# Gate and up projections as seven half products for eight, tokens in two groups, on one core

## The reference, cut to what matters

```python
def rmsnorm(x, g):
    r = lax.rsqrt(jnp.mean(xf * xf, axis=-1, keepdims=True) + EPS)
    return xf * r * g

def swiglu(hn, w_gate_up, w_down):
    gate, up = jnp.split(hn @ w_gate_up, 2, axis=-1)
    return (jax.nn.silu(gate) * up) @ w_down

h = h + swiglu(rmsnorm(h, norm_ffn_g), w_gate_up, w_down)
return rmsnorm(h, norm_final_g)
```

## Time and profile before

| | us |
|---|---|
| median of 3 runs | 2632.27 |
| lowest and highest | 2631.83, 2634.83 |
| the profiled execution: time | 2631.12 |
| the profiled execution: span from its first to its last instruction | 2629.4 |
| PE busy | 2526.4 |
| DVE busy | 1284.7 |
| ACT busy | 546.5 |
| POOL busy | 283.7 |

### The profile page before, as it was taken

The page is one execution under the profiler, slowest core; times in us unless marked ns, Lnnn a source line. Parts: engine busy times, 40 slices in busy tenths (PEclk is TensorE's granted clock), DMA queues, the critical chain, the costliest instruction groups (busy, mean ns, idle before and its releaser), DMA issues.

```text
span 2629.4 us, 31047 instructions
## 1 busy us (share of the span) xinstructions
PE 2526.4 (96%) x11282; PEld 2056.1 (78%) x11282; DVE 1284.7 (49%) x2113; ACT 546.5 (21%) x733; POOL 283.7 (11%) x238
## 2 busy tenths in 40 slices
PE   6899999799999999999999999999999999999994
PEld 4688887688888788888768888888888888888883
DVE  6634553368880784352442554434434434433437
ACT  5301110322221432130331321111111111111122
POOL 3278870000000220000000000000000000000001
PEclk9999999999999999999999999999999999999997
DMA  5432227532226642222310000000000000000002
GB/s 191 133 117 99 86 74 156 146 122 80 80 80 168 200 175 76 84 96 80 104 57 32 32 33 32 33 32 32 32 32 32 32 32 32 32 32 32 32 16 96
DMA packets 87288, 201.27 MB, mean 77 GB/s; under 512 B 12608, under 2 KB 41792, under 8 KB 87232
## 3 DMA queue, kind: packets, MB, share of 16 engines
q1 hardware_dynamic: 83872, 189.01, 22.2%
q0 software_dynamic: 3360, 11.54, 1.4%
HBM read 148.64 MB, written 53.97 MB: 77 GB/s over the span
## 4 chain that ended last, share of the span: by engine, by line
PE 90%; DVE 3%; DMA 2%; issue 2%; POOL 1%; ACT 1%; SPq 0%; DVEq 0%; POOLq 0%; ACTq 0%
PE bank L616 28%; PE bank L617 28%; PE bank L618 28%; PE bank L893 2%; PE bank L839 1%; PE bank L870 1%; DMA BBL<-scratch_BB 1%; POOL ACC L515 1%; DMA scratch_CO<-COS 1%; DVE HR L1774 1%; PE bank L836 0%; DVE ACC L1613 0%; PE bank L713 0%; PE bank L882 0%; PE bank L781 0%
## 5 line engine op out<-in xcount | busy, mean ns | idle before, releaser
L616 PE MATMUL bank<-XN,WLO 128*128 128x512 f32 x2400 | 935.5, 390 | 3.1 <-DVE XN L1711 1.7
L617 PE MATMUL bank<-XN,WHI 128*128 128x512 f32 x2400 | 933.8, 389 | 0.0
L618 PE MATMUL bank<-XN,WHI 128*128 128x512 f32 x2400 | 933.7, 389 | 0.0
L616 PEld LDWEIGHTS bank<-XN,WLO 128*128 128x128 f32 x2400 | 450.4, 188 | 98.8 <-issue 5.1
L617 PEld LDWEIGHTS bank<-XN,WHI 128*128 128x128 f32 x2400 | 450.5, 188 | 94.2 <-issue 1.0
L618 PEld LDWEIGHTS bank<-XN,WHI 128*128 128x128 f32 x2400 | 450.4, 188 | 93.9
L948 ACT ACTIVATE WHI<-WR 128x1024 fp32r<-128x1024 f32 x150 | 157.7, 1051 | 603.1 <-PE bank L618 537.3
L1243 DVE TENSOR_TENSOR WLO<-WR,WHI 128x1024 fp32r<-128x1024 f32 x150 | 197.8, 1319 | 126.3 <-ACT WHI L948 118.0
L1758 DVE TENSOR_TENSOR HR<-bank,HR 128x512 f32<-128x512 f32 x264 | 181.8, 691 | 126.9 <-PE bank L618 125.0
L616 PE MATMUL bank<-AF,WLO 128*128 128x512 f32 x528 | 208.2, 394 | 0.7 <-DVE HR L1758 0.7
L617 PE MATMUL bank<-AF,WHI 128*128 128x512 f32 x528 | 208.0, 394 | 0.0
(11 more groups left out here) (200 smaller groups left out, 2526.4 us busy)
## 6 DMA issues: line engine op xcount, KB each, us to landing
WR<-W_all SPq DMA_DIRECT2D x150, 512.0 KB, 3.3
scratch_G<-GS SPq DMA_DIRECT2D x16, 768.0 KB, 3.8
XS<-xT SPq DMA_DIRECT2D x8, 768.0 KB, 4.9
scratch_CO<-COS SPq DMA_DIRECT2D x8, 768.0 KB, 4.1
COL<-scratch_CO SPq DMA_DIRECT2D x8, 768.0 KB, 4.3
G2L<-scratch_G SPq DMA_DIRECT2D x8, 768.0 KB, 5.8
G1L<-scratch_G SPq DMA_DIRECT2D x8, 768.0 KB, 7.2
XR<-xT SPq DMA_DIRECT2D x8, 768.0 KB, 4.3
```

The costliest lines, as they stand in the source:

```text
L616: pe_mm(out, w[1], x[0], start=first, stop=False)
L617: pe_mm(out, w[0], x[1], start=False, stop=False)
L618: return pe_mm(out, w[0], x[0], start=False, stop=last)
```

## The change

The FFN is written anew, on all engines. What it does:

- **Two groups.** The tokens are two groups of 768 (`GRP`), each two halves of 384 (`HB`). Each group goes through the whole FFN (all weights are loaded twice), group 0 first.
- **Normalised first.** `XO` loses `last_pair`; after it come the sums, the roots and Newton steps for the norm, and then the inputs: four quarters B11, B21 (first half of the tokens, k-tiles 0 to 3 and 4 to 7) and the like for the second half are made by DVE as `HR` times gain times `RB` (`normed`, 4 operations of 384 columns each), and combined (`T1` to `T4`, 1536 columns each). ACT copies each of the seven into its high part `XH` (`x_hi`), DVE subtracts for the low part `XL` (`x_lo`, which signals `x_ready`).
- **Seven products for eight.** For one tile of gate and up (a step), the 2 x 2 block product (gate and up by the two halves of k; the two halves of the tokens) is made by Strassen's scheme in Winograd's form with seven half products, each 4 k-tiles x 3 matmuls of 384 columns. Their weights are `entries`: three are halves of loaded weights, four are combinations `SW0` to `SW3` that DVE makes, 128 x 512 each. Each entry is split by ACT (`entry_hi`) and DVE (`entry_lo`) into a ring of six.
- **Four banks for the products.** Products 0, 2 share bank 0, products 1, 3 bank 1, products 4, 6 bank 2, product 5 bank 3. A first product's value is read out (ACT copies bank 0 to `S1T`; DVE sums bank 1 and `S1T` to `U2T`, and after product 3 to `U3T`) before the next adds onto the bank. `UP2`, `UP1` and `G2T` are sums with these.
- **Down** uses banks 4 to 7: per chunk and group 4 entries, 96 matmuls of 384 columns, and 16 additions of 384 columns to `HR` by DVE.
- **Final norm.** Group 0's squares and sum are taken in the first step of group 1, its scaling (`y_first`, 8 operations of 768 columns) in the last pair of group 1, and it is stored then. Only group 1's 768 tokens remain for the end.
- **Places.** The seven pairs `XH`, `XL` and `AF` lie in SBUF where `XN` lay, the ring where `XN`'s end, `WR`, `WHI` and `WLO` lay. `AF` lay above before.

Core of the diff:

```diff
+    B11, T2, B21, T3, T1, T4, B22 = range(7)
+PRODUCTS = ((0, B11), (1, T2), (0, B21), (1, T3), (2, T1), (3, T4), (2, B22))
...
+    AF = low("AF", 84, [2, 2, GRP], F32R)
+    RINGS = (96, 104, 112, 100, 108, 116)
...
     @block.tensor
-        slots("xo", 3, K8, xin)
-        last_pair("xo", 2)
+        slots("xo", 4, K8, xin)
+        sums(2, ACC2)
...
+        def ffn_step(n, p, s, g, first=False):
+            for j, (bk, op) in enumerate(PRODUCTS):
+                pe.wait_ge(S("entry_lo"), n + j + 1)
+                if first:
+                    pe.wait_ge(S("x_ready"), 7 * g + j + 1)
...
+                if j == 2:
+                    pe.wait_ge(S("first_kept"), s + 1)
+                if j == 3:
+                    pe.wait_ge(S("summed"), 5 * s + 1)
+                if j == 4 and not (first and g == 0):
+                    pe.wait_ge(S("summed"), 5 * s)
+                if j == 6:
+                    pe.wait_ge(S("summed"), 5 * s + 3)
+                fresh = j in (0, 1, 4, 5)
+                for a in range(HT):
+                    last = product(PS[bk][:, 0:HB], factors((p + j) % RINGF, a), (XH[op][:, a, :], XL[op][:, a, :]),
+                                   fresh and a == 0, a == HT - 1, not fresh)
+                last.then_inc(S("products"), 1)
...
+            ffn_step(n, 0, s, g, first=True)
+            ffn_step(n + 7, 1, s + 1, g)
+            def pair(i):
+                ffn_step(n + PAIR0 + 18 * i, 2, s + 2 + 2 * i, g)
+                down(n + PAIR0 + 7 + 18 * i, 3, d + i)
+                ffn_step(n + PAIR0 + 11 + 18 * i, 1, s + 3 + 2 * i, g)
...
     @block.vector
+        def ffn_step(n, p, s, odd, rg, ru, follow, rd, ng, nu, i, fresh=False, head=False):
+            for j in range(7):
+                if j == 1:
+                    with_first(U2T, 1, S1T, (S("first_kept"), s + 1), j, s)
+                if j == 3:
+                    with_first(U3T, 1, S1T, (S("first_kept"), s + 1), j, s)
+                if j == 4:
+                    with_first(UP2, 2, U3T, (S("summed"), 5 * s + 2), j, s)
+                if j == 5:
+                    with_first(UP1, 3, U3T, (S("summed"), 5 * s + 2), j, s)
+                if j == 6:
+                    with_first(G2T, 2, U2T, (S("summed"), 5 * s + 1), j, s)
+                if j == 0:
+                    next_lo(6, n + 6, q, s, rg, ru, i)
+                elif follow == "S":
+                    next_lo(j - 1, n + 6 + j, q, s + 1, ng, nu, i)
+                elif j < 5:
+                    entry_lo(n + 6 + j, q, down_operand(j - 1, rd))
...
+                if j in (1, 2) and not fresh:
+                    gated(s - 1, j - 1)
+                if j == 3 and not fresh:
+                    gated_lo(s - 1, 1 - odd, 0)
+                    gated_lo(s - 1, 1 - odd, 1)
```

More of the change, by code:

```diff
@@ L478, in _ @@
                 load_memory(h)
-        with loop(nc.sync, 4) as i:
+        with loop(nc.sync, 3) as i:
             for par in range(2):
                 weights(SLOT0["xo"] + par + 2, par, i)
[L482 to L492, removed]
@@ L712, in sums @@
                     pe.wait_ge(S("rms"), NB * norm + 1)
-                nc.tensor.matmul(sums_bank(norm, b)[:], ones[:], acc[:, blk(b)], start=True, stop=True
+                nc.tensor.matmul(sums_bank(b)[:], ones[:], acc[:, blk(b)], start=True, stop=True
                                  ).then_inc(S("sums"), 1)
@@ L968, in roots @@
                 act.wait_ge(S("sums"), NB * norm + b + 1)
[L969 removed]
+                root(RB[:, blk(b)], sums_bank(b)[:]).then_inc(S("root"), 1)
         act.wait_ge(raw[0], 16)
@@ new lines, in down, with x_hi, final_square @@
+        def down(n, p, s, d, ng, nu, i):
+            for m in range(4):
+                act.wait_ge(S("down_made"), 16 * d + 4 * m + 4)
+                next_hi(2 + m, n + 6 + m, (p + 6 + m) % RINGF, s, ng, nu, i)
+        def x_hi(g, j):
+            act.wait_ge(S("x_made"), 4 * g + min(j + 1, 4))
+            copy(XH[j][:], XF[j][:]).then_inc(S("x_high"), 1)
+        def final_square(g, k, out):
+            act.wait_ge(S("down_added"), 16 * (CHUNKS * (g + 1) - 1) + 2 * (k + 1))
+            if g == 0 and k:
+                act.wait_ge(S("final_added"), k)
+            nc.scalar.activation(out[:], HR[:, k, g * GRP:(g + 1) * GRP], ACT.Square).then_inc(S("final_squares"), 1)
@@ L1763, in _, with xo_pair @@
-        chunk(0)
-        with V.Fori(1, CHUNKS - 1) as c:
-            chunk(c)
-        then(V.memset(ACC2[:], 0.0))
-        chunk(CHUNKS - 1, final=True)
-        for b in range(NB):
-            dve.wait_ge(S("root"), NB * 3 + b + 1)
-            newton(RB[:, blk(b)], sums_bank(3, b)[:], NT).then_inc(S("rms"), 1)
-            dve.wait_ge(S("rms"), NB * 3 + b + 1)
+        then(V.memset(ACC2[:], 0.0))
+        def xo_pair(i):
+            for par in range(2):
+                j = 2 * i + par
+                if not (isinstance(i, int) and i == 3 and par):
+                    lo(SLOT0["xo"] + par + 1, 2 * i)
+                for b in range(NB):
+                    h = one(HR, j)[:, blk(b)]
+                    V.tensor_tensor(h, take(RES0["xo"] + NB * par + b, i, 2 * NB), h, ALU.add).then_inc(evac, 1)
+                if par or not (isinstance(i, int) and i == 0):
+                    add_squares(2, j - 1, SQ2[:, 1 - par, :])
@@ new lines, in _ @@
+        then(V.memset(FA[:], 0.0))
+        for m in range(4):
+            down_add(2 * CHUNKS - 1, 1, m)
+            if m:
+                final_add(1, 2 * m - 2, FSQ[:, 2 * m - 2, :])
+                final_add(1, 2 * m - 1, FSQ[:, 2 * m - 1, :])
+        final_add(1, KT - 2, FSQ[:, KT - 2, :])
+        final_add(1, KT - 1, FSQ[:, KT - 1, :])
+        for b in range(2):
+            dve.wait_ge(S("root"), NB * 3 + 2 + b + 1)
+            newton(RB[:, gcol(1, b)], sums_bank(b)[:, 0:HB], NT).then_inc(S("rms"), 1)
+            dve.wait_ge(S("rms"), NB * 3 + 2 + b + 1)
```

512 lines of the change are left out of this document (395 added, 117 removed).

## The result

| | before | changed |
|---|---|---|
| median, us | 2632.05 (2630.49 to 2634.83, 4 runs) | 2647.78 (2646.75 to 2648.93, 4 runs) |
| profiled span, us | 2629.4 | 2646.7 |
| start of XO in the profiled execution, us | 1365.11 | 1370.26 |
| end of XO to the end of the span, us | 1133.6 | 1145.8 |

The ratio is 1.0059, 95% interval 1.0041 to 1.0076: slower by more than the 0.2% that can be told from no change. The forecast was 2626, a small gain. The range to 2660 holds the result, but the direction was forecast wrongly.

What follows compares the result with a forecast made beforehand. PE, busy 96%, bounds the kernel. After XO, 1007.1 us of matmuls plus 40.9, 14.4, 25.3, 2.2, 6.8, 1.0, 3.6, 3 and 23.3 give 1127.6 against 1133.7, hence 2626 us; range 2606 to 2660.

Steps and rivals of the forecast that it cites:

- group 0's norm: In group 1: 2.2 us for additions in its first step, and 2.2 for two norm sums and late Newton steps.
- `y_first`: Late in group 1: eight DVE operations, 7.7 us, delay the down additions, with 0.9 us of slack: 6.8 us.
- tail: From the last product to the end of the span: 41.9 us now, 23.3 us after the change.
- Part 1, matmuls: FFN on PE: 5808 matmuls of 384 columns at 173.4 ns take 1007.1 us, 80.7 less than now.
- B: FFN matmuls: surcharge goes with the columns, starts 170.0 ns apart; faster, 2616 us; chance 0.25.
- C: FFN matmuls: AF's surcharge everywhere, starts 180 ns apart; slower, 2655 us; chance 0.10.
- D: FFN matmuls: no surcharge to speak of, 162.7 ns; faster, 2595 us; chance 0.04.
- Part 2, step stalls: Steps followed by another step: product 6 waits 0.7 us for DVE's UP2, 20 times, 14.4 us.
- restarts: PE starts slower after a wait: 33 waits of 0.11 us, 3.6 us in all.
- Rival A: DVE operations do not run back to back; each long step stalls 1.5 to 2 us; about +30, 2656 us; chance 0.18.
- Part 3, start seam: After XO: DVE needs 47 us before product 3 of step 0, PE covers 6.2; cost 40.9 us.
- Part 4, group seam: Between the groups: DVE needs 46 us, PE has 22.9; cost 23.1 plus 2.2 in the first step, 25.3 us.

Runs made afterwards that it cites:

- both moves: Changed kernel with SW2, SW3 and the third entry after UP2, and one y_first per pass of group 1's loop: 2614.93 us, ratio 0.993.
- the third norm later: On top of both moves, the Newton step of the ffn norm's third block goes from the start seam to just before step 2: 2610.96 us, ratio 0.9911.

## Why the prediction was right or wrong

**The step that failed is the sizing of PE's waits for DVE: three terms, 14.4 for the steps, 2.2 for group 0's norm behind step 22 and 6.8 for `y_first`, measured 23.7, 8.3 and 10.3.** They are 18.9 us too low together, and the start and group seams and the tail are 6.2 more. Where PE waits, and for what, was mostly forecast rightly; the norm's term also had its reason wrong (below). The forecast of 6.1 us gain, out of 81 saved and 75 spent, stood on terms that were nearly all too low. The part from XO's end that is not matmuls was put at 120.5 us; 5% more would have turned the sign, and it was 15% more.

- **Part 1, matmuls: right.** 1007.1 forecast, 1006.7 measured. A surcharge per matmul holds for 384 columns: B (170.0), C (180) and D (162.7) are out. That it comes from the weight load was a guess, and no run here tests it. `AF` has the lower surcharge too, 13.3 ns for 20, as forecast from its new place; since its width changed as well, the place is not shown to be the cause.
- **Part 2, step stalls: the place was right, the size too small.** Product 6 waits for `UP2`, and moving three operations removes it. 17.8 us over 19 such steps, 0.94 each and not 0.72, since the stretch takes 9.2 to 9.3 us and not 9.0; 2.2 more at the next step's first product (gone too once the order is changed); and 2.4 in the steps that a down part follows, which stay when the order is changed and were in no term. 22.3 in all against 14.4 and most of the restarts. Rival A is out: it needed 1.5 to 2 us in each. The measured 2648 lies nearer to A's 2656 than to the forecast, but not for A's reason.
- **Part 3, start seam: right within 3 us.** Product 3 started at +48.25 against 47, and took 3.9 us at half clock instead of 2.08. What was not seen: ACT's queue, with `S1T` behind everything, gave nearly the same time, so that 2.65 us less on DVE moved product 3 by 1.6 only.
- **Part 4, group seam: right within 2 us** (product 3 of step 22 47.2 after the last step, 46 forecast), with a clock that fell here as well (0.80).
- **Group 0's norm: the term that failed worst in proportion.** 2.2 in step 22 and 2.2 after it were forecast; leaving it out saved 4.4 in step 22, 1.9 in step 23 and 5.5 in step 24 with its down part. Steps 22 and 23 already stall for DVE, so little could lie beside PE. The Newton steps were priced as "0.9 late", as if a step had DVE time to spare wherever they stood; but they stand ahead of `U2T` and behind a root that DVE waits for. Placed two steps later, in steps that do not stall, the same norm cost 11.4.
- **`y_first`: 10.3 for 6.8**, of which 2.7 are matmuls at the 1.2 GHz level after the wait (granted clock 0.50 from 2574.36 to 2580.25). The forecast allowed 3 us of clock for the seams together and none here.
- **Tail: 24.6 for 23.3.** The parts were right, 24.5 in sum; the 1.2 us subtracted for an overlap of the Newton steps did not occur. In the chain of waits of the changed kernel, as in the earlier trace rows, the second Newton step begins when the six normalisations behind the first have ended:

```profile
2627.03 1.66 PE bank L1030 x2
2628.72 0.59 ACT RB L1076
2629.33 0.57 DVE NT L1466
...
2631.51 4.74 DVE HR L2202 x6
2636.24 0.48 DVE NT L1466
```

Summed from the table: start seam +2.9, steps +9.3, group seam +1.7, norm +6.1, `y_first` +3.5, last down and tail +1.6, less the 6.6 that the forecast held apart: 18.5 us, and 0.4 back on the matmuls. Of the signs that the forecast named, the starts, product 3 near +47 and the late product 6 came; "PE idle near 90 us" was 98 (1145.8 less 1047.5 busy); "DVE above 80% busy between the seams" did not come. It was 72%, which is also the most that the forecast's own counts allow (12.7, 10.3 and 10.0 us of DVE work in two steps and a down part of 45.8 us of PE), and at 72% the steps did stall for DVE. What stays open: the further 3 to 4 us between the medians (15.7) and the part from XO's end (12.2). Over all thirteen profiled executions (the two given, and eleven runs) the median less that part is 1498.4 to 1502.0 us, so it is no more than the scatter of a profiled execution against its median, but it was not tried separately.

## What to carry to other kernels

Price work that is added to an engine by the operation behind it that another engine waits for, and not by the engine's sum of work. A block ahead of such an operation cost about its whole length or more, even in steps with DVE time to spare (`y_first` in one block, 7.4 us for 10.3; the Newton steps, 4.1 for 5.5; the norm moved two steps later, 11.4). The same `y_first` as single operations of 0.95 us, one behind each down part, cost nothing that shows. Before giving up a change that spends what it saves, look at what stands ahead of the operation that frees the waiting engine: one reordering of three operations was worth 20.7 us, and the kernels with both moves and the third norm later take 2611 us, 0.9911 of the kernel before (0.9896 to 0.9926). And measure a change from a point common to both traces: 5.1 of the 17.3 us by which the span grew lie ahead of it, and the same code varied there by 7 us from one profiled execution to another.

## What the runs showed of the hardware that was not expected

- The surcharge of 13.3 ns on a matmul is the same at 384 columns (`XH`, `AF`) and at 512 (`XN`; `AF` had 20 there), and is absent at half clock: starts 0.32 us apart for 384 columns, 320 ns being 384 columns at 1.2 GHz. The Trainium skill's cold rule (page "TensorE: Matmul & The Clock Gate", section "Back-to-back issue gap", N/1.2) agrees with the trace, its warm one does not.
- A wait of 7 us cost up to 2.9 us more than itself in matmuls at half clock, and matmuls of no use in the waits kept the granted clock at 0.96 where it was 0.61. Nothing was won by them here, since the last filling was longer than its wait.
- A root just ahead of a loop put two table loads into the body of the loop, one of them ahead of a plain copy; they cost 16 us over seven passes, in most of them 2.1 of the 2.57 us that they take.
